# The first weight chunk in two halves, and a projection loop in which each tile's product stands ahead of a later tile's transposes

## The chip, the cores and the metric

The kernel runs on one core of a Trainium2 chip. The metric is the device time of one execution in microseconds, here of a single core. TensorE (PE in the rows) multiplies, VectorE (DVE) and ScalarE (ACT) work on the tiles elementwise, GpSimd (POOL) does small vectors and constants, and SyncE (SP) issues DMAs. Each engine runs its own instruction list in order and waits on semaphores.

## The reference, cut to what matters

The whole is one decoder layer with attention, an mLSTM and a mixture of experts. The change touches its first stage alone, the input projection:

```
def rmsnorm(x, w):
    y = xf * lax.rsqrt(jnp.mean(xf * xf, axis=-1, keepdims=True) + EPS)
    return y * w
xn = rmsnorm(x, p["attn_norm_w"])     # 1024 prompt tokens and 64 sample tokens, 1024 wide
proj = xn @ p["w_in"]                 # w_in: 1024 x 4872, float32; this stage makes 2824 columns of it
```

The product is made to float32 accuracy from operands split into a high part (rounded to the fp32r type) and a low part (the remainder): high by high, high by low, low by high are added up in one PSUM bank.

## The kernel before

`project` is the stage. The tokens are 9 tiles: tiles 0 to 7 of 128 prompt tokens, tile 8 of the 64 sample tokens. The weight comes in chunks of 352 columns (chunk 0 has 8 more, the gate columns, so 360) and 1024 rows, which are KD = 8 slices `k` of 128. Two sets of buffers (`w_ring`, `w_hi`, `w_lo`) alternate between chunks. Nothing plans the order: each engine's list is written out by hand in its block.

Per token tile t of chunk 0 these steps follow one another, each on its engine:

- ScalarE `square(t)` (L281), then GpSimd two short operations for the reciprocal root, then ScalarE `scale(t)` (L287) on the x tile.
- TensorE turns the tile: 8 transposes (L534), four into bank 6 and four into bank 7. I call this turn(t).
- VectorE `turned(t)` (L390, two instructions) multiplies both banks by the norm weight into `f_tile`.
- ScalarE `feat_hi(t)` (L291) casts to `f_hi`; VectorE `feat_lo(t)` (L402) subtracts for `f_lo`. Tile 8 has extra copies for `f_side` (L295, L401).
- TensorE product(t): 24 matmuls (L522 to L524, 8 slices by 3) of tile t with chunk 0 into PSUM bank t modulo 3. It first waits for `free` of that bank, which is only given back when the tile three before has been copied out by `evacuate` (L187 and L193, release at L198).

The copies out of chunk 0 are placed in the loops: ScalarE copies tile 0, 2, 4 in its passes t = 4, 6, 8 after `scale(t)`, VectorE tile 1 in its pass t = 5 and tile 3 in its pass t = 7, and both the rest after their loops. In a VectorE pass before: `turned(t)`, then `feat_lo(t - 1)`, then the copy, and in pass 7 then `split_lo(1)` (L408), the low part of chunk 1. ScalarE's pass is `square(t)`, `feat_hi(t - 1)`, `scale(t)`, the copy, and in pass 7 `split_hi(1)`.

TensorE's list before is turn(0), turn(1), turn(2), product(0), turn(3), product(1), and so on to turn(8), product(6), product(7), product(8). Seven more chunks of nine products follow, on two alternating sets of three banks. SyncE's list starts with x tiles 0 and 1, the norm weight, chunk 0 whole (L218), x tiles 2 to 8, chunk 1, and small loads.

Of the kernel before, what the change touches and what calls it, by code (L numbers as in the profile page):

```python
# [19 lines left out]
F32 = mybir.dt.float32  # L20
# [4 lines left out]
ALU = mybir.AluOpType  # L25
# [86 lines left out]
def project(nc, a, S):  # L112

    with ExitStack() as ctx:
# [62 lines left out]
        with nc.Block() as block:  # L177
# [37 lines left out]
            def _(sp):  # L215
                def load(n):
                    v = n % 2
                    sp.dma_start(w_ring[v][:, :, 0:width[n != 0]], w_view[:, :, columns(n, width[n != 0])]).then_inc(w_loaded[v], 16)  # L218
# [8 lines left out]
                for t in range(NT + 1):  # L227
                    src = xs if t == NT else a["x_prompt"][0, t * P:(t + 1) * P, :]
                    sp.dma_start(x_tile[t][:tile_rows(t)], src).then_inc(x_loaded[t], 16)
                    if t == 1:  # L230
                        sp.dma_start(S["attn_nw"][:], a["attn_norm_w"][0].rearrange("(k p) -> p k", p=P)).then_inc(norm_w_loaded, 16)
                        load(0)
                load(1)
                for dst, src in ((ib[:], a["mlstm_i_bias"].rearrange("o h -> h o")), (fb[:], a["mlstm_f_bias"].rearrange("o h -> h o")),
                                 (m0[:], a["state_m"][0].rearrange("b h -> h b")),
# [7 lines left out]
                spare = a["expert_rows"][(NE - 1) * SLOTS:MAXB * SLOTS, :].rearrange("(b s) d -> s b d", s=SLOTS)  # L243
                sp.wait_ge(zeros_ready, 1)
                for n in range(NCH - 2):
                    sp.wait_ge(w_lo_ready[n % 2], n // 2 + 1)
                    load(n + 2)
                    store(n)
                    if n in (1, 2):
                        half = slice((n - 1) * D // 2, n * D // 2)  # L250
                        sp.dma_start(spare[:, :, half], bc(zeros[:], 1, MAXB - NE + 1)).then_inc(spare_filled, 16)
# [1 line left out]
                sp.dma_start(a["row_c"], r_i[:]).then_inc(rows_stored, 16)  # L253
                sp.dma_start(a["m_prompt"][0, 0].rearrange("(h o) -> h o", o=1), r_m[:, TP - 1:TP]).then_inc(rows_stored, 16)
                sp.dma_start(a["m_sample"][0].rearrange("b h -> h b"), m_last[:, 8:16]).then_inc(rows_stored, 16)
                sp.wait_ge(w_lo_ready[0], NCH // 2)
                for j in range(2):
                    sp.dma_start(S["wg"][j][:], w_view[:, :, CG + j * P:CG + (j + 1) * P]).then_inc(wg_loaded[j], 16)
                store(NCH - 2)
# [17 lines left out]
            def _(act):  # L277
# [20 lines left out]
                def split_hi(n):  # L298
# [27 lines left out]
                square(1)  # L326
                scale(0)
                scale(1)
                feat_hi(0, P)
                split_hi(0)  # L330
                for t in range(2, NT + 1):
                    square(t)
                    feat_hi(t - 1, P)
# [43 lines left out]
            def _(dve):  # L377
# [26 lines left out]
                def split_lo(n):  # L404
                    cc, v = n // 2, n % 2
                    w = width[n != 0]
                    dve.wait_ge(w_hi_ready[v], cc + 1)
                    dve.tensor_tensor(w_lo[v][:, :, 0:w], w_ring[v][:, :, 0:w], w_hi[v][:, :, 0:w].bitcast(F32), ALU.subtract).then_inc(w_lo_ready[v], 1)  # L408

                rows = Own(dve, row_step)  # L410
                first = lambda ap: ap[:, TP:T:ST]
# [55 lines left out]
                            dve.tensor_copy(dst[:, :, q, :], src).then_inc(gcol_ready, 1)  # L467
                    dve.tensor_copy(S["wprev_all"][:], banks[7][:, 448:512]).then_inc(gcol_ready, 1)

                for t in range(NT + 1):  # L470
                    turned(t, tile_rows(t))
                    if t:
                        feat_lo(t - 1, P)
                    if t == 1:
                        split_lo(0)
                    if t in (5, 7):
                        evacuate(dve, 1, dve.tensor_copy, 0, only=t - 4)
                    if t == 7:
                        split_lo(1)
                feat_lo(NT, TS)  # L480
                for n in range(NCH):
                    if n == 3:
                        max_rows()
# [20 lines left out]
            def _(pe):  # L504
                pe.wait_ge(ms_ready, 6)

                def product(cc, v, t, w=CW):

                    b, r = 3 * v + t % 3, tile_rows(t)
                    pe.wait_ge(free[b], 3 * cc + t // 3 + 1)  # L510
                    if t == NT:
                        for k in range(KD):
                            if k:
                                pe.matmul(banks[b][:r, :w], f_hi[:, k, TP:T], w_lo[v][:, k, 0:w], start=False, stop=False)
                            ins = pe.matmul(banks[b][:, :w], f_side(slice(k, k + 1)).rearrange("p o t -> p (o t)"), w_hi[v][:, k, 0:w], start=(k == 0), stop=(k == KD - 1))
                            if k == 0:
                                pe.matmul(banks[b][:r, :w], f_hi[:, k, TP:T], w_lo[v][:, k, 0:w], start=False, stop=False)
                        ins.then_inc(full[b], 1)
                        return
                    for k in range(KD):  # L520
                        hi, lo = (f[:, k, t * P:t * P + r] for f in (f_hi, f_lo))
                        pe.matmul(banks[b][:r, :w], hi, w_hi[v][:, k, 0:w], start=(k == 0), stop=False)  # L522
                        pe.matmul(banks[b][:r, :w], hi, w_lo[v][:, k, 0:w], start=False, stop=False)  # L523
                        ins = pe.matmul(banks[b][:r, :w], lo, w_hi[v][:, k, 0:w], start=False, stop=(k == KD - 1))  # L524
                    ins.then_inc(full[b], 1)

                for t in range(NT + 1):
                    r = tile_rows(t)
                    pe.wait_ge(xn_ready, t + 1)
                    for h in range(2):  # L530
                        pe.wait_ge(xt_free[h], t + 1)
                        for k in range(4):
                            c = (4 * h + k) * P
                            ins = pe.transpose(banks[6 + h][:, k * P:k * P + r], x_tile[t][:r, c:c + P], S["ident"][:r, :r])  # L534
                        ins.then_inc(xt_full[h], 1)
                    if t >= 2:
                        if t == 2:
                            pe.wait_ge(w_lo_ready[0], 1)
                        pe.wait_ge(f_lo_ready, t - 1)
                        product(0, 0, t - 2, width[0])  # L540
                for t in range(NT - 1, NT + 1):
                    pe.wait_ge(f_lo_ready, t + 1)
                    product(0, 0, t, width[0])
# [2211 lines left out]
```

## Time and profile before

| | us |
|---|---|
| runs (3): median, lowest, highest | 1500.71, 1497.29, 1501.1 |
| the profiled execution: its own time | 1498.19 |
| its span, first to last instruction | 1496.4 |
| TensorE busy in it | 1415.3 (95%) |
| VectorE, ScalarE, GpSimd busy | 1003.0, 726.7, 210.4 |
| mean granted TensorE clock | 0.982 |

The span counts from the first to the last instruction, and the execution's own time has 1.8 us around it. The share of busy time is an average over stages; for a change in the first 60 us one reads the timeline of the engines there.

### The profile page before, as it was taken

How to read it: one execution, taken by the hardware profiler on the slowest of the kernel's cores; microseconds unless marked ns; L12 is line 12 of the kernel's file. 1: busy time of each engine (PE TensorE's matmuls, PEld its weight loads, DVE VectorE, ACT ScalarE, POOL GpSimd, SP SyncE). 2: the span in 40 equal slices, each digit the busy share in tenths (PEclk: the TensorE clock that was granted, in tenths of full speed). 3: DMA queues.
4: the chain of work that ended last, by engine and by line, in shares of the span. 5: the costliest groups of instructions: out<-in, count | busy, mean ns of one | idle time of the engine just before them, and what ended most of it. 6: DMA issues, size and time to landing. Idle time of an engine off the chain costs nothing.

```text
span 1496.4 us, 21540 instructions
## 1 busy us (share of the span) xinstructions
PE 1415.3 (95%) x8054; PEld 1198.2 (80%) x8054; DVE 1003.0 (67%) x1341; ACT 726.7 (49%) x861; POOL 210.4 (14%) x243
## 2 busy tenths in 40 slices
PE   5999999999999999999999889999999999999990
PEld 5999999998999998899788666777777777777760
DVE  4522321166666668776576688888888888888875
ACT  6421121144444444423212247777777777777760
POOL 2600000021111111000200040231111111111014
PEclk9999999999999999999999899999999999999995
DMA  6336423243333323658721289999999999999938
GB/s 200 120 123 212 147 79 70 76 136 109 119 124 114 115 73 108 190 179 252 282 92 42 97 332 392 365 380 399 394 390 391 390 390 393 396 393 399 379 126 319
DMA packets 135895, 347.40 MB, mean 232 GB/s; under 512 B 13768, under 2 KB 92044, under 8 KB 110160
## 3 DMA queue, kind: packets, MB, share of 16 engines
q1 hardware_dynamic: 125672, 312.32, 57.8%
q0 software_dynamic: 6048, 21.50, 4.7%
q10 hardware_dynamic: 4120, 12.85, 2.2%
q8 instruction: 34, 0.56, 0.2%
q14 instruction: 21, 0.17, 0.0%
HBM read 292.34 MB, written 55.28 MB: 232 GB/s over the span
## 4 chain that ended last, share of the span: by engine, by line
PE 45%; DVE 3%; DMA 1%; ACT 1%; issue 1%; POOL 0%; POOLq 0%; ACTq 0%; DVEq 0%
PE xt_ey L2560 4%; PE xt_ey L2561 4%; PE xt_ey L2562 4%; PE y_h_up L2539 4%; PE y_h_up L2538 4%; PE y_h_up L2540 4%; PE logits_gate L2538 2%; PE logits_gate L2540 2%; PE logits_gate L2539 2%; PE ranks_gate L2538 2%; PE ranks_gate L2540 2%; PE ranks_gate L2539 2%; PE y_x L2527 2%; DVE e_w_lo L2419 1%; PE y_x L2084 1%; PE y_h_up L2084 1%
## 5 line engine op out<-in xcount | busy, mean ns | idle before, releaser
L2419 DVE TENSOR_TENSOR e_w_lo<-mixed,e_w_hi 128x2048 fp32r<-128x2048 f32 x64 | 145.8, 2297 | 0.5 <-ACT e_w_hi L2352 0.5
L2419 DVE TENSOR_TENSOR e_w_lo<-w_out,e_w_hi 128x2048 fp32r<-128x2048 f32 x64 | 143.5, 2282 | 2.9 <-ACT e_w_hi L2352 2.9
L987 PE MATMUL gate_banks<-f_hi,wg_hi 128*128 128x364 f32 (+1 forms) x376 | 126.8, 337 | 0.9 <-DVE wg_lo L855 0.5
L2352 ACT CAST e_w_hi<-mixed 128x2048 fp32r<-128x2048 f32 x62 | 117.0, 1912 | 14.0 <-ACT e_y_rows L2373 8.9
L988 PE MATMUL gate_banks<-f_lo,wg_hi 128*128 128x364 f32 (+1 forms) x376 | 123.5, 328 | 0.0
L989 PE MATMUL gate_banks<-f_hi,wg_lo 128*128 128x364 f32 (+1 forms) x376 | 123.4, 328 | 0.0
L2352 ACT CAST e_w_hi<-w_out 128x2048 fp32r<-128x2048 f32 x64 | 121.8, 1904 | 0.6 <-ACT e_y_rows L2373 0.6
L2560 PE MATMUL xt_ey<-e_w_hi,e_hT_hi 128*96 128x512 f32 x256 | 103.5, 404 | 5.1 <-DVE e_w_lo L2419 3.9
L2279 POOL CAST idx<-token_of_slot 96x1 uint32 (+1 forms) x30 | 48.4, 1614 | 402.2 <-PE y_x L2527 368.9
L2561 PE MATMUL xt_ey<-e_w_lo,e_hT_hi 128*96 128x512 f32 x256 | 101.9, 398 | 0.0
L2538 PE MATMUL y_h_up<-e_w_hi,e_x_hi 128*96 128x512 f32 x256 | 100.8, 394 | 0.7 <-DVE e_w_lo L2419 0.7
L2562 PE MATMUL xt_ey<-e_w_hi,e_hT_lo 128*96 128x512 f32 x256 | 101.0, 395 | 0.0
L2539 PE MATMUL y_h_up<-e_w_lo,e_x_hi 128*96 128x512 f32 x256 | 100.8, 394 | 0.0
L2540 PE MATMUL y_h_up<-e_w_hi,e_x_lo 128*96 128x512 f32 x256 | 100.6, 393 | 0.0
L522 PE MATMUL gate_banks<-w_hi,f_hi 128*128 128x352 f32 (+1 forms) x256 | 84.1, 329 | 1.1 <-ACTq L198 1.1
L522 PE MATMUL pj<-w_hi,f_hi 128*128 128x352 f32 x256 | 82.7, 323 | 1.8 <-ACTq L198 1.8
L524 PE MATMUL gate_banks<-w_hi,f_lo 128*128 128x352 f32 (+1 forms) x256 | 83.4, 326 | 0.0
L523 PE MATMUL gate_banks<-w_lo,f_hi 128*128 128x352 f32 (+1 forms) x256 | 83.3, 326 | 0.0
L523 PE MATMUL pj<-w_lo,f_hi 128*128 128x352 f32 x256 | 82.9, 324 | 0.0
L524 PE MATMUL pj<-w_hi,f_lo 128*128 128x352 f32 x256 | 82.7, 323 | 0.0
L2419 DVE TENSOR_TENSOR e_w_lo<-w_gate,e_w_hi 128x2048 fp32r<-128x2048 f32 x32 | 72.9, 2280 | 1.2 <-ACT e_w_hi L2352 1.2
L2419 DVE TENSOR_TENSOR e_w_lo<-w_up,e_w_hi 128x2048 fp32r<-128x2048 f32 x32 | 71.9, 2287 | 0.1
(626 smaller groups left out, 3604.6 us busy)
## 6 DMA issues: line engine op xcount, KB each, us to landing
w_out<-in_w_down_e SPq DMA_DIRECT2D x64, 1024.0 KB, 8.0
mixed<-in_w_gate_e SPq DMA_DIRECT2D x32, 1024.0 KB
mixed<-in_w_up_e SPq DMA_DIRECT2D x32, 1024.0 KB, 8.4
w_gate<-in_w_gate_e SPq DMA_DIRECT2D x32, 1024.0 KB, 7.2
w_up<-in_w_up_e SPq DMA_DIRECT2D x32, 1024.0 KB
expert_rows<-e_y_rows ACTq DMA_DIRECT2D x32, 384.0 KB, 7.3
proj<-mixed SPq DMA_DIRECT2D x8, 1408.0 KB, 5.6
w_ring<-in_w_in SPq DMA_DIRECT2D x7, 1408.0 KB, 10.7
```

The lines of the kernel that those rows point to most:

```text
L522: pe.matmul(banks[b][:r, :w], hi, w_hi[v][:, k, 0:w], start=(k == 0), stop=False)
L523: pe.matmul(banks[b][:r, :w], hi, w_lo[v][:, k, 0:w], start=False, stop=False)
L524: ins = pe.matmul(banks[b][:r, :w], lo, w_hi[v][:, k, 0:w], start=False, stop=(k == KD - 1))
L987: pe.matmul(bank, wg_hi[j][:, k, :], hi, start=(k == 0), stop=False)
L2352: act.copy(hi(i, step, j), raw(i, u, j)).then_inc(hi_ready[i], 1)
L2419: dve.tensor_tensor(lo(i, u, j), raw(i, u, j), hi(i, step, j).bitcast(F32), ALU.subtract).then_inc(lo_ready[i], 1)
L2538: pe.matmul(bank[:SLOTS, :], x_hi[u][:, k, :], w_hi[:, n, :], start=(k == 0), stop=False)
L2539: pe.matmul(bank[:SLOTS, :], x_hi[u][:, k, :], w_lo[:, n, :], start=False, stop=False)
L2540: ins = pe.matmul(bank[:SLOTS, :], x_lo[u][:, k, :], w_hi[:, n, :], start=False, stop=(k == KD - 1))
L2560: pe.matmul(Y[:SLOTS, cols], h_hi[:, f, :], w_hi[:, n, cols], start=(f == 0), stop=False)
L2561: pe.matmul(Y[:SLOTS, cols], h_hi[:, f, :], w_lo[:, n, cols], start=False, stop=False)
L2562: ins = pe.matmul(Y[:SLOTS, cols], h_lo[:, f, :], w_hi[:, n, cols], start=False, stop=(f == KF - 1))
```

## The change

Four edits, all in chunk 0 of the projection.

1. SyncE loads chunk 0 as two DMAs, k slices 0 to 3 and 4 to 7, the first with a semaphore of its own. ScalarE and VectorE split it by the same halves. The counts of the semaphores for buffer set 0 go up by one, because chunk 0 now signals twice.
2. ScalarE's list starts scale(1), first half of `w_hi`, `feat_hi(0)`, second half. Its loop is unchanged.
3. VectorE: tile t's `feat_lo` now follows its own `turned(t)` in the same pass. The copies of tile 1 and tile 3 stay in passes 5 and 7, behind it.
4. TensorE: product(t) now stands ahead of turn(t + 2), and product(0) waits for the halves of `w_lo` at k = 0 and k = 4.

```diff
+        FIRST_HALVES = (slice(0, KD // 2), slice(KD // 2, KD))
...
                     if t == 1:
                         sp.dma_start(S["attn_nw"][:], a["attn_norm_w"][0].rearrange("(k p) -> p k", p=P)).then_inc(norm_w_loaded, 16)
-                        load(0)
+                        for i, ks in enumerate(FIRST_HALVES):
+                            sp.dma_start(w_ring[0][:, ks, 0:width[0]], w_view[:, ks, columns(0, width[0])]).then_inc(w_loaded[0] if i else first_half_loaded, 16)
...
+                def first_split_hi(i):
+                    ks = FIRST_HALVES[i]
+                    act.wait_ge(w_loaded[0] if i else first_half_loaded, 16)
+                    act.copy(w_hi[0][:, ks, 0:width[0]], w_ring[0][:, ks, 0:width[0]]).then_inc(w_hi_ready[0], 1)
...
                 scale(1)
+                first_split_hi(0)
                 feat_hi(0, P)
-                split_hi(0)
+                first_split_hi(1)
                 for t in range(2, NT + 1):
...
+                def first_split_lo(i):
+                    ks = FIRST_HALVES[i]
+                    dve.wait_ge(w_hi_ready[0], i + 1)
+                    dve.tensor_tensor(w_lo[0][:, ks, 0:width[0]], w_ring[0][:, ks, 0:width[0]], w_hi[0][:, ks, 0:width[0]].bitcast(F32), ALU.subtract).then_inc(w_lo_ready[0], 1)
...
-                for t in range(NT + 1):
+                turned(0, P)
+                first_split_lo(0)
+                feat_lo(0, P)
+                first_split_lo(1)
+                turned(1, P)
+                feat_lo(1, P)
+                for t in range(2, NT + 1):
                     turned(t, tile_rows(t))
-                    if t:
-                        feat_lo(t - 1, P)
-                    if t == 1:
-                        split_lo(0)
+                    feat_lo(t, tile_rows(t))
                     if t in (5, 7):
                         evacuate(dve, 1, dve.tensor_copy, 0, only=t - 4)
                     if t == 7:
                         split_lo(1)
-                feat_lo(NT, TS)
...
                     for k in range(KD):
+                        if first and k % (KD // 2) == 0:
+                            pe.wait_ge(w_lo_ready[0], k // (KD // 2) + 1)
...
-                    if t >= 2:
-                        if t == 2:
-                            pe.wait_ge(w_lo_ready[0], 1)
-                        pe.wait_ge(f_lo_ready, t - 1)
-                        product(0, 0, t - 2, width[0])
+                turn_x(0)
+                turn_x(1)
+                for t in range(NT - 1):
+                    pe.wait_ge(f_lo_ready, t + 1)
+                    product(0, 0, t, width[0], t == 0)
+                    turn_x(t + 2)
                 for t in range(NT - 1, NT + 1):
                     pe.wait_ge(f_lo_ready, t + 1)
                     product(0, 0, t, width[0])
```

TensorE at the start, from turn(1) on (banks pj6 and pj7 take the transposes, the gate banks the products). Before:

```order
L534 MATMUL pj6<-ident,mixed 128x128 [waits xt_free0,xn_ready]
L534 MATMUL pj6<-ident,mixed 128x128 x3
L534 MATMUL pj7<-ident,mixed 128x128 [waits xt_free1]
L534 MATMUL pj7<-ident,mixed 128x128 x3
L534 MATMUL pj6<-ident,mixed 128x128 [waits xt_free0,xn_ready]
L534 MATMUL pj6<-ident,mixed 128x128 x3
L534 MATMUL pj7<-ident,mixed 128x128 [waits xt_free1]
L534 MATMUL pj7<-ident,mixed 128x128 x3
L522 MATMUL gate_banks<-w_hi0,f_hi_49 128x360 [waits pj_free0,f_lo_ready,w_lo_ready0]
```

The same place in the changed kernel:

```order
L553 MATMUL pj6<-ident,mixed 128x128 [waits xt_free0,xn_ready]
L553 MATMUL pj6<-ident,mixed 128x128 x3
L553 MATMUL pj7<-ident,mixed 128x128 [waits xt_free1]
L553 MATMUL pj7<-ident,mixed 128x128 x3
L541 MATMUL gate_banks<-w_hi0,f_hi_49 128x360 [waits w_lo_ready0,pj_free0,f_lo_ready]
```

Turn(2) has moved from ahead of product(0) to behind it.

VectorE's first instructions (early holds `f_tile`). Before:

```order
L390 TENSOR_TENSOR early<-pj6,attn_nw 128x512 [waits xt_full0,norm_w_loaded]
L390 TENSOR_TENSOR early<-pj7,attn_nw 128x512 [waits xt_full1]
L390 TENSOR_TENSOR early<-pj6,attn_nw 128x512 [waits xt_free1,xt_full0]
L390 TENSOR_TENSOR early<-pj7,attn_nw 128x512 [waits xt_full1]
L402 TENSOR_TENSOR f_lo_50<-early,f_hi_49 128x8x128 [waits xt_free1,f_hi_ready]
L408 TENSOR_TENSOR w_lo0<-w_ring0,w_hi0 128x2880 [waits w_hi_ready0]
```

Changed:

```order
L400 TENSOR_TENSOR early<-pj6,attn_nw 128x512 [waits xt_full0,norm_w_loaded]
L400 TENSOR_TENSOR early<-pj7,attn_nw 128x512 [waits xt_full1]
L423 TENSOR_TENSOR w_lo0<-w_ring0,w_hi0 128x1440 [waits xt_free1,w_hi_ready0]
L412 TENSOR_TENSOR f_lo_50<-early,f_hi_49 128x8x128 [waits f_hi_ready]
L423 TENSOR_TENSOR w_lo0<-w_ring0,w_hi0 128x1440 [waits w_hi_ready0]
L400 TENSOR_TENSOR early<-pj6,attn_nw 128x512 [waits xt_full0]
L400 TENSOR_TENSOR early<-pj7,attn_nw 128x512 [waits xt_full1]
```

Tile 0 is finished, and both halves of the weight's low part made, before tile 1's banks are read.

TensorE around product(4), which needs bank 1 back from tile 1 (`pj_free1`). Before, what stands ahead of it is turn(6):

```order
L524 MATMUL gate_banks<-w_hi0,f_lo_50 128x360
L534 MATMUL pj6<-ident,mixed 128x128 [waits xt_free0,xn_ready]
L534 MATMUL pj6<-ident,mixed 128x128 x3
L534 MATMUL pj7<-ident,mixed 128x128 [waits xt_free1]
L534 MATMUL pj7<-ident,mixed 128x128 x3
L522 MATMUL gate_banks<-w_hi0,f_hi_49 128x360 [waits pj_free1,f_lo_ready]
```

Changed, it is turn(5):

```order
L543 MATMUL gate_banks<-w_hi0,f_lo_50 128x360
L553 MATMUL pj6<-ident,mixed 128x128 [waits xt_free0,xn_ready]
L553 MATMUL pj6<-ident,mixed 128x128 x3
L553 MATMUL pj7<-ident,mixed 128x128 [waits xt_free1]
L553 MATMUL pj7<-ident,mixed 128x128 x3
L541 MATMUL gate_banks<-w_hi0,f_hi_49 128x360 [waits pj_free1,f_lo_ready]
```

Every product stands one turn earlier in TensorE's list than before. VectorE's pass 5, which reads turn(5) and then copies out tile 1, is in the changed kernel:

```order
L400 TENSOR_TENSOR early<-pj6,attn_nw 128x512 [waits xt_full0,f_lo_ready]
L400 TENSOR_TENSOR early<-pj7,attn_nw 128x512 [waits xt_full1]
L412 TENSOR_TENSOR f_lo_50<-early,f_hi_49 128x8x128 [waits xt_free1,f_hi_ready]
L190 COPY mixed<-gate_banks 128x352 [waits pj_full1]
L196 COPY if_tok_73<-gate_banks 128x2x4
```

Before it has the same five forms in this pass, but its f_lo is that of tile 4; now it is that of tile 5, whose banks the two instructions ahead of it have just read.

## Rows read from the trace of the kernel before

**Rows 1.** The page: busy time, share and instructions of each engine.

```profile
PE 1415.3 (95%) x8054; PEld 1198.2 (80%) x8054; DVE 1003.0 (67%) x1341; ACT 726.7 (49%) x861; POOL 210.4 (14%) x243
```

**Rows 2.** Timeline, TensorE: start us, length us, instruction [idle before <-releaser].

```profile
8.57 3.98 PE L534 MATMUL pj<-ident,mixed 128*128 128x128 f32 x16 [8.57 <-ACT mixed L287]
19.97 1.97 PE L534 MATMUL pj<-ident,mixed 128*128 128x128 f32 x8 [7.42 <-ACT mixed L287]
21.59 0.65 PE L522 MATMUL gate_banks<-w_hi,f_hi 128*128 128x360 f32 x1
...
23.49 0.33 PE L522 MATMUL gate_banks<-w_hi,f_hi 128*128 128x360 f32 x1
```

**Rows 3.** Timeline, TensorE: turn(3), product(1), turn(4).

```profile
26.47 1.04 PE L534 MATMUL pj<-ident,mixed 128*128 128x128 f32 x8
27.26 0.41 PE L522 MATMUL gate_banks<-w_hi,f_hi 128*128 128x360 f32 x1
...
31.29 1.04 PE L534 MATMUL pj<-ident,mixed 128*128 128x128 f32 x8
```

**Rows 4.** Timeline, TensorE: turn(7), turn(8), product(6).

```profile
45.77 1.03 PE L534 MATMUL pj<-ident,mixed 128*128 128x128 f32 x8
...
51.06 0.71 PE L534 MATMUL pj<-ident,gate_rows 64*128 64x64 f32 x8 [0.30 <-ACT gate_rows L287]
51.70 0.43 PE L522 MATMUL gate_banks<-w_hi,f_hi 128*128 128x360 f32 x1
```

**Rows 5.** DMA issues of the first 25 us: KB, median us from issue to landing.

```profile
w_ring<-in_w_in SPq DMA_DIRECT2D x1, 1440.0 KB, 8.5
```

**Rows 6.** Timeline, ScalarE, 0 to 75 us.

```profile
11.33 1.04 ACT L291 CAST f_hi<-early 128x1024 fp32r<-128x1024 f32 x1 [1.82 <-DVEq L395]
12.28 2.59 ACT L304 CAST w_hi<-w_ring 128x2880 fp32r<-128x2880 f32 x1
...
28.62 1.05 ACT L291 CAST f_hi<-early 128x1024 fp32r<-128x1024 f32 x1 [2.67 <-DVEq L395]
29.57 1.15 ACT L287 ACTIVATE mixed<-mixed,x_rstd 128x1024 f32<-128x1024 f32 x1
...
48.72 1.05 ACT L291 CAST f_hi<-early 128x1024 fp32r<-128x1024 f32 x1
...
55.01 0.71 ACT L295 CAST f_side<-early 128x448 fp32r<-128x448 f32 x2 [0.70 <-DVE f_lo L402]
```

**Rows 7.** Timeline, VectorE, 0 to 75 us.

```profile
9.77 1.47 DVE L390 TENSOR_TENSOR early<-pj,attn_nw 128x512 f32<-128x512 f32 x2 [9.77 <-PE pj L534]
...
13.43 1.23 DVE L402 TENSOR_TENSOR f_lo<-early,f_hi 128x1024 fp32r<-128x1024 f32 x1 [0.15 <-DVE early L390]
14.90 3.16 DVE L408 TENSOR_TENSOR w_lo<-w_ring,w_hi 128x2880 fp32r<-128x2880 f32 x1 [0.24 <-ACT w_hi L304]
...
27.18 1.29 DVE L390 TENSOR_TENSOR early<-pj,attn_nw 128x512 f32<-128x512 f32 x2 [3.14 <-PE pj L534]
...
39.42 0.52 DVE L187 COPY mixed<-gate_banks 128x352 f32<-128x352 f32 x1
...
47.93 1.23 DVE L402 TENSOR_TENSOR f_lo<-early,f_hi 128x1024 fp32r<-128x1024 f32 x1 [0.15 <-DVE early L390]
...
49.84 3.09 DVE L408 TENSOR_TENSOR w_lo<-w_ring,w_hi 128x2816 fp32r<-128x2816 f32 x1 [0.18 <-DVE if_tok L193]
52.85 0.75 DVE L390 TENSOR_TENSOR early<-pj,attn_nw 128x256 f32<-128x256 f32 x2
...
56.64 0.68 DVE L402 TENSOR_TENSOR f_lo<-early,f_hi 128x512 fp32r<-128x512 f32 x1
```

**Rows 8.** Timeline, TensorE: the first matmul after a wait.

```profile
721.85 0.47 PE L2073 MATMUL y_x<-w_out_hi,first_merged_hi 128*128 128x512 f32 x1 [2.49 <-PEq L103]
```

**Rows 9.** Windows: length, PE, PEld, DVE, ACT, POOL busy, clock, DMA.

```profile
720.00:724.00 4.00, 2.15 (x8) 1.77 (x9) 1.75 (x3) 2.17 (x3) 1.98 (x10) 0.90 0.15 7
724.00:728.00 4.00, 4.00 (x14) 3.18 (x13) 4.00 (x5) 3.61 (x4) 3.46 (x9) 0.68 0.78 165
```

More of the change, by code:

```diff
@@ L156, in project @@
         w_loaded = [sem(f"w_loaded{v}") for v in range(2)]
+        first_half_loaded = sem("first_half_loaded")
         full = [sem(f"pj_full{b}") for b in range(6)]
@@ L245, in _ @@
                 for n in range(NCH - 2):
-                    sp.wait_ge(w_lo_ready[n % 2], n // 2 + 1)
+                    sp.wait_ge(w_lo_ready[n % 2], n // 2 + 2 - n % 2)
                     load(n + 2)
@@ L255, in _ @@
                 sp.dma_start(a["m_sample"][0].rearrange("b h -> h b"), m_last[:, 8:16]).then_inc(rows_stored, 16)
-                sp.wait_ge(w_lo_ready[0], NCH // 2)
+                sp.wait_ge(w_lo_ready[0], NCH // 2 + 1)
                 for j in range(2):
@@ L406, in split_lo @@
                     w = width[n != 0]
-                    dve.wait_ge(w_hi_ready[v], cc + 1)
+                    dve.wait_ge(w_hi_ready[v], cc + 2 - v)
                     dve.tensor_tensor(w_lo[v][:, :, 0:w], w_ring[v][:, :, 0:w], w_hi[v][:, :, 0:w].bitcast(F32), ALU.subtract).then_inc(w_lo_ready[v], 1)
+                def first_split_lo(i):
+                    ks = FIRST_HALVES[i]
+                    dve.wait_ge(w_hi_ready[0], i + 1)
+                    dve.tensor_tensor(w_lo[0][:, ks, 0:width[0]], w_ring[0][:, ks, 0:width[0]], w_hi[0][:, ks, 0:width[0]].bitcast(F32), ALU.subtract).then_inc(w_lo_ready[0], 1)
                 rows = Own(dve, row_step)
@@ L505, in _, with product @@
                 pe.wait_ge(ms_ready, 6)
-                def product(cc, v, t, w=CW):
+                def product(cc, v, t, w=CW, first=False):
                     b, r = 3 * v + t % 3, tile_rows(t)
@@ L525, in product, with turn_x @@
                     ins.then_inc(full[b], 1)
-                for t in range(NT + 1):
+                def turn_x(t):
                     r = tile_rows(t)
@@ L553, in _ @@
                     for v in range(2):
-                        pe.wait_ge(w_lo_ready[v], cc + 1)
+                        pe.wait_ge(w_lo_ready[v], cc + 2 - v)
                         for t in range(NT + 1):
@@ L557, in _ @@
                 for v in range(2):
-                    pe.wait_ge(w_lo_ready[v], NCH // 2)
+                    pe.wait_ge(w_lo_ready[v], NCH // 2 + 1 - v)
                     for t in range(NT + 1):
```

## The prediction

> **What bounds the kernel now.** I read the page first: TensorE is busy for 95% of the span [rows 1]. What the change can give or take is therefore time in which TensorE stands still in the first 64 us, since every later stage is fed by buffers that TensorE's own progress sets free; a shift of its list there should arrive at the end at full size. Next the timeline of TensorE. Turn(0) and turn(1) run from 8.57 to 12.55, then it idles 7.42 us until scale(2) on ScalarE lets turn(2) start at 19.97; product(0) starts at 21.59 [rows 2]. From then on it is nearly full: turn(3) starts at 26.47, product(1) at 27.26, turn(4) at 31.29, so in steady state a turn takes 0.79, a product 4.03 and a step of both 4.82 us [rows 3]. Turn(8) waits 0.30 us and takes 0.64 [rows 4].
>
> **The gain at the start.** ScalarE ends scale(1) at 9.5, the end of the piece ahead of the row at 11.33. The whole chunk lands about 8.5 us after its issue at 2.2, so at 10.7 [rows 5]; the landing of its first half no row shows. It is at the latest 10.7; at an even rate over the 2.5 MB of x tiles 0 and 1 and the chunk, its 1.8 MB would be there near 8. I take anything before 9.5, when ScalarE comes free. Half of `w_hi` costs 1.39 us, by the line through 1.04 us for 1024 elements and 2.59 for 2880 [rows 6], half of `w_lo` 1.66 by 1.23 and 3.16 [rows 7]. Walk: first `w_hi` half 9.5 to 10.9; `turned(0)` 9.77 to 11.24 [rows 7]; `feat_hi(0)` 11.33 to 12.4, second `w_hi` half to 13.7; on VectorE first `w_lo` half 11.3 to 13.0, `feat_lo(0)` 12.9 to 14.15, second half 14.1 to 15.7, `turned(1)` 15.7 to 17.1. So product(0) starts at 14.2, not 21.59, and its k = 4 wait, 3.6 us in, finds the half of 15.7 done. If the first half landed only at 10.7, product(0) would start at 15.0: 0.8 us less gain.
>
> Its length: before, 6 of its first pitches fill 21.59 to 23.49 at about 0.30 us, and after 23.49 they are 0.165 (18 to 26.47) [rows 2, 3]; that is 1.2 against 2.4 GHz, and the faster level came 3.5 us after turn(2) began. The same 3.5 us from 14.2 on gives 11 slow matmuls, and 13 fast ones end at 19.9. At the slow level throughout it would end at 21.6, so 0 to 1.7 us are open; I take 19.9, as the row is the only ramp there is here. Scale(2) stands behind `feat_hi(1)` (17.1 to 18.15) and ends at 19.2, so turn(2) does not wait. Turn(3) then starts at 19.9 + 0.79 + 4.03 = 24.7. Before, at 26.47, TensorE had product(1) still to do; so it is 1.8 + 4.0 = 5.8 us ahead.
>
> **The steady step.** `turned(t)` starts 0.71 after turn(t) (27.18 against 26.47), `feat_hi(t)` 2.15 after it (28.62), scale(t + 1) ends 4.25 after it (29.57 + 1.15) [rows 3, 6, 7]. Now `feat_lo(t)` follows `feat_hi(t)`: start at 3.23, end at 4.46, and product(t), which needs it, is due at 4.82 + 0.79 = 5.61. Both fit. The extra DMA issue (about 0.5 us of SyncE) delays x tiles 2 to 8 and the small loads behind it; what covers it is that scale(2) has over 2 us of slack behind `feat_hi(1)`. Uncovered it would cost 0.5. The two more instructions on ScalarE and VectorE are in the walk.
>
> **Where the lead is lost: the bank handed back late.** Product(4) needs bank 1, which VectorE releases in pass 5 after copying out tile 1. Before, product(4) stands behind turn(6), and the copy ran at 39.42, behind `feat_lo(4)` [rows 7], while turn(6) began only at 31.29 + 2 x 4.82 = 40.9. Changed, product(4) stands behind turn(5), and the copy behind `feat_lo(5)`, which cannot start before turn(5) + 3.23. From the start of a `feat_lo` to the release is 1.91 us (47.93 to 49.84, with the same copies in pass 7) [rows 7]. So bank 1 is free at turn(5) + 5.15, product(4) starts at 5.2 and was due at 0.79: **4.4 us of standing still**. The queue behind it on TensorE is all the rest, and VectorE and ScalarE can't shorten it, since what they wait for is turn(5) itself.
>
> Product(6) needs bank 0 from tile 3, copied in pass 7 behind `feat_lo(7)`. Here ScalarE does chunk 1's `w_hi` and square(8) ahead of `feat_hi(7)`, which starts 2.95 after turn(7) (48.72 against 45.77) [rows 4, 6]. `Feat_lo(7)` starts at 4.03, the release is at 5.94, product(6) starts at 6.0 and was due at 0.79: **5.2 us**. Turn(8) waits no more: 0.3 us back.
>
> Product(8) needs bank 2 from tile 5, which VectorE copies after `feat_lo(8)`. `Split_lo(1)` (3.1 us) ends at turn(7) + 9.0, before turn(8) is through, so `turned(8)` starts at turn(8) + 0.4. From there to the start of `feat_lo(8)` were 3.79 us (52.85 to 56.64), of which 0.70 was a wait that has gone [rows 6, 7]; `feat_lo(8)` is 0.55 shorter, so the release comes 3.09 + 1.36 later, at turn(8) + 4.85 and 0.1 to act. Product(8) was due at 0.64 + 4.03 = 4.67: **0.3 us**, with bounds 0 and 1.
>
> **The sum at full clock.** Turn(5) at 24.7 + 2 x 4.82 = 34.4; product(4) 39.6; turn(7) 39.6 + 4.03 + 4.82 = 48.4; product(6) 54.4; turn(8) 58.4; product(7) 59.1; product(8) 63.4. Before, product(8) began at 51.70 + 2 x 4.03 = 59.8 [rows 4]. So +3.6 us (-5.8 + 4.4 + 5.2 + 0.3 - 0.3 and rounding).
>
> **The clock after a standstill.** At 721.85 TensorE resumes after a wait of 2.49 us, and the granted clock of the two 4 us windows there is 0.90 and 0.68 [rows 8, 9]. Between levels 1 and 0.5 that is 0.8 + 2.6 = 3.4 us at 1.2 GHz, almost all while it worked, half of it lost: 1.6 us. The standstills of 4.4 and 5.2 us are longer, so I charge 1.6 for each, +3.2; bounds 0 and 3.2. The second is not hidden by the first: each slow stretch lies inside the product that follows its wait, and the next wait is counted from a turn behind it. The sum is +3.6 + 3.2 = +6.8 us.
>
> The Trainium skill, "TensorE: Matmul & The Clock Gate", "What's actually happening", says that "the default state is throttled, and activity releases the throttle". By that rule a bubble costs more than its length, which speaks against this change; without it the sum would be +3.6, with it +6.8. The trace agrees at its wait of 2.49 us, with a clock of 0.68 behind it.
>
> **Against the runs.** The profiled execution took 1498.19 us, its span 1496.4; the median is 1500.71, 2.5 above the former. The difference carries over: 1498.2 + 6.8 = 1505.0 for such an execution, 1507.5 for the median. About 0.3%, 4.5 us, is what a measurement of this kernel can tell from no change.
>
> **Cases.**
> - A, forecast, 0.62: both waits with their slow stretches, +6.8: 1507.5.
> - B, 0.17: the waits are as worked out, but the clock stays at 2.4 GHz after one or both, or the falls are short: +3.6 to +5.2, near 1505. For it: TensorE has been working densely up to each wait. Against it: the fall behind 2.49 us.
> - C, 0.10: the start gains less, because the first half lands late (0.8) or product(0) runs at 1.2 GHz throughout (1.7), or a slow stretch is longer: +8 to +10, near 1509.5.
> - D, the other side, 0.08: the bank handover does not decide, because the releases come within 0.8 us of turn(5) and turn(7). That needs the copy of tile 1 to run ahead of `feat_lo(5)`, and it decides at a release before turn + 0.8. Then product(6) is due at 24.7 + 4 x 4.82 + 0.79 = 44.8, product(7) at about 49.9, and product(8) still waits for `feat_lo(8)`, which `split_lo(1)` holds back to some 13.3 after turn(7) (9.0 + 4.3), so to 57.3 against 59.8: -2.5, 1498.2. Even then most of the 5.8 us is given back. The order of VectorE's list speaks against it.
> - E, 0.03: the whole lead reaches the end, -5.8: 1494.9. It needs D and no wait at product(8).
>
> Faster by over 0.3% is E: 0.03. Within 0.3% are D and half and more of B with a little of A: 0.23. Slower by over 0.3%: 0.74. The range takes in B and C: from +2 to +11 us with the scatter of the medians, 1502.5 to 1511.5.
>
> **What would show it.** In the changed profile: product(0) near 14.2 and turn(3) near 24.7; TensorE idle about 4.4 us behind turn(5), released by VectorE's release behind the copy of tile 1, and about 5.2 us behind turn(7); matmul pitches of 0.30 us behind both and a granted clock under 1 there; the first matmul of product(8) near 66.6. A TensorE timeline without idle between 20 and 60 us would make it wrong, as would a later stage in which the delay shrinks.

## The result

The changed kernel took 1508.32 us (median of 5 runs, 1506.24 to 1511.57), the kernel before 1499.02 (5 runs, 1497.29 to 1501.1). The ratio is 1.0057, with a 95% interval of 1.0046 to 1.0068: slower by 8.5 us (6.9 to 10.2). The two medians lie 9.3 us apart; the differences below go by the ratio. The profiled execution took 1508.32 us, its span 1506.6, which is 10.2 above the span before.

The page of the changed kernel, to be held against [rows 1]:

```profile
PE 1423.9 (95%) x8054; PEld 1205.8 (80%) x8054; DVE 1001.5 (66%) x1342; ACT 726.3 (48%) x862; POOL 220.8 (15%) x243
```

TensorE is busy for as large a share as before, with the same 8054 matmuls, and 8.6 us longer. That is the first sign that it not only stood still but ran slower. The timeline of TensorE (start us, length us, instruction, idle before it and who ended it), against [rows 2 to 4], first the start:

```profile
14.21 0.67 PE L541 MATMUL gate_banks<-w_hi,f_hi 128*128 128x360 f32 x1 [1.69 <-DVE f_lo L412]
14.68 0.50 PE L542 MATMUL gate_banks<-w_lo,f_hi 128*128 128x360 f32 x1
...
18.22 0.33 PE L542 MATMUL gate_banks<-w_lo,f_hi 128*128 128x360 f32 x1
...
20.04 1.04 PE L553 MATMUL pj<-ident,mixed 128*128 128x128 f32 x8
```

Product(0) begins at 14.21 in place of 21.59. Its matmuls are 0.30 us apart up to 17.98 and 0.165 from 18.22 on. Turn(2) follows at once at 20.04. Then turn(3), turn(5) and product(4):

```profile
24.88 1.04 PE L553 MATMUL pj<-ident,mixed 128*128 128x128 f32 x8
...
34.53 1.03 PE L553 MATMUL pj<-ident,mixed 128*128 128x128 f32 x8
39.72 0.64 PE L541 MATMUL gate_banks<-w_hi,f_hi 128*128 128x360 f32 x1 [4.16 <-DVEq L201]
```

Turn(6), turn(7) and product(6), whose releaser is the same:

```profile
46.34 1.03 PE L553 MATMUL pj<-ident,mixed 128*128 128x128 f32 x8
...
51.16 1.04 PE L553 MATMUL pj<-ident,mixed 128*128 128x128 f32 x8
57.14 0.64 PE L541 MATMUL gate_banks<-w_hi,f_hi 128*128 128x360 f32 x1 [4.95 <-DVEq L201]
```

Turn(8), product(7), product(8), and the first matmul of chunk 1:

```profile
63.69 0.71 PE L553 MATMUL pj<-ident,gate_rows 64*128 64x64 f32 x8
...
68.70 0.40 PE L532 MATMUL gate_banks<-w_hi,f_side 128*128 128x360 f32 x1 [0.17 <-DVEq L201]
...
71.40 0.32 PE L541 MATMUL pj<-w_hi,f_hi 128*128 128x352 f32 x1
```

In the kernel before, that last row was:

```profile
62.32 0.32 PE L522 MATMUL pj<-w_hi,f_hi 128*128 128x352 f32 x1
```

So chunk 1 begins 9.1 us later. Who was waited for, by TensorE in the first 85 us (total us, times, longest us):

```profile
PE gate_banks L541 <- DVEq L201: 9.1, 2, 4.9
...
PE gate_banks L532 <- DVEq L201: 0.2, 1, 0.2
```

L201 is the release of a bank on VectorE. The two waits of 4.2 and 4.9 us stand ahead of product(4) and product(6), the one of 0.2 us ahead of product(8).

The windows of the changed kernel (stretch, length, busy time of PE, PEld, DVE, ACT and POOL, granted clock, DMA share, GB/s), against [rows 9]:

```profile
12.00:16.00 4.00, 2.31 (x9) 1.91 (x8) 4.00 (x4) 2.70 (x4) 1.15 (x2) 1.00 1.03 412
36.00:40.00 4.00, 0.28 (x1) 0.31 (x2) 2.27 (x4) 3.19 (x5) 0.00 (x0) 0.83 0.00 0
40.00:44.00 4.00, 4.00 (x14) 4.00 (x14) 0.00 (x0) 0.46 (x2) 0.74 (x2) 0.50 0.00 0
44.00:48.00 4.00, 4.00 (x24) 3.97 (x24) 0.95 (x2) 0.00 (x0) 0.00 (x0) 0.82 0.00 0
52.00:56.00 4.00, 0.19 (x2) 0.00 (x0) 1.98 (x3) 3.97 (x5) 1.71 (x5) 0.96 0.00 0
56.00:60.00 4.00, 2.86 (x10) 2.89 (x11) 3.82 (x4) 0.59 (x3) 3.84 (x3) 0.50 0.87 273
60.00:64.00 4.00, 4.00 (x21) 3.77 (x21) 0.19 (x1) 0.00 (x0) 3.62 (x6) 0.69 0.27 94
```

With each wait the granted clock is at its lower level for 6.8 us: 0.17 of 4 us twice over, then a whole 4 us, then 0.18 twice over make 1.4 + 4.0 + 1.4, and the second fall likewise 0.3 + 4.0 + 2.5. Counted back from the whole windows, the clock fell at about 38.6 and 55.7, so that some 1.1 and 1.5 us of the low stretches lay still inside the waits, which ended at 39.72 and 57.14. Product(4) takes 6.62 us up to turn(6), product(6) 6.55 up to turn(8); the steady product took 4.03 [rows 3].

VectorE (against [rows 7]), then ScalarE (against [rows 6]), at the places of the sum:

```profile
11.36 1.66 DVE L423 TENSOR_TENSOR w_lo<-w_ring,w_hi 128x1440 fp32r<-128x1440 f32 x1
12.94 1.22 DVE L412 TENSOR_TENSOR f_lo<-early,f_hi 128x1024 fp32r<-128x1024 f32 x1
...
37.76 1.23 DVE L412 TENSOR_TENSOR f_lo<-early,f_hi 128x1024 fp32r<-128x1024 f32 x1 [1.22 <-ACT f_hi L295]
38.90 0.52 DVE L190 COPY mixed<-gate_banks 128x352 f32<-128x352 f32 x1
39.33 0.16 DVE L196 COPY if_tok<-gate_banks 128x8 f32<-128x8 f32 x1
...
55.18 1.22 DVE L412 TENSOR_TENSOR f_lo<-early,f_hi 128x1024 fp32r<-128x1024 f32 x1 [2.02 <-ACT f_hi L295]
```

```profile
9.39 1.38 ACT L313 CAST w_hi<-w_ring 128x1440 fp32r<-128x1440 f32 x1
```

The first half of `w_hi` starts at 9.39, with no idle time ahead, so the half had landed; the first half of `w_lo` runs 11.36 to 13.0 and `feat_lo(0)` at 12.94. The release of bank 1 comes after `feat_lo(5)` at 37.76 and the copies at 38.90 and 39.33, and TensorE starts at 39.72, within 0.3 us. `Feat_lo(7)` starts at 55.18, 4.02 us after turn(7) as forecast.

### The profile page after: what moved, and what is told of

Its sections match the earlier page's. It is cut to its first block, busy times and chain, and to the rows that moved or that the text cites. A ratio compares the mean times of both kernels' runs of the same rounds, so it can differ in the third digit from the quotient of the medians.

```text
span 1506.6 us, 21545 instructions
## 1 busy us (share of the span) xinstructions
PE 1423.9 (95%) x8054; PEld 1205.8 (80%) x8054; DVE 1001.5 (66%) x1342; ACT 726.3 (48%) x862; POOL 220.8 (15%) x243
## 4 chain that ended last, share of the span: by engine, by line
PE 45%; DVE 3%; DMA 1%; ACT 1%; issue 1%; POOL 0%; POOLq 0%; ACTq 0%; DVEq 0%
PE xt_ey L2581 4%; PE xt_ey L2582 4%; PE xt_ey L2583 4%; PE y_h_up L2560 4%; PE y_h_up L2559 4%; PE y_h_up L2561 4%; PE logits_gate L2559 2%; PE logits_gate L2561 2%; PE logits_gate L2560 2%; PE ranks_gate L2559 2%; PE ranks_gate L2561 2%; PE ranks_gate L2560 2%; PE y_x L2548 2%; DVE e_w_lo L2440 1%; PE y_x L2105 1%; PE y_h_up L2105 1%
## 5 line engine op out<-in xcount | busy, mean ns | idle before, releaser
L541 PE MATMUL gate_banks<-w_hi,f_hi 128*128 128x352 f32 (+1 forms) x256 | 87.0, 340 | 11.9 <-DVEq L201 9.1
L1008 PEld LDWEIGHTS gate_banks<-f_hi,wg_hi 128*128 128x128 f32 x376 | 70.7, 188 | 1.6 <-issue 1.4
```

The lines of the kernel that those rows point to most:

```text
L1008: pe.matmul(bank, wg_hi[j][:, k, :], hi, start=(k == 0), stop=False)
```

## Experiments

All are timed against the kernel before in alternating rounds. The last column is the ratio less 1, times 1499 us. The column ahead of it compares the first recorded matmul of chunk 1 with that of before (62.32) in one profiled execution each. (A matmul record can be missing from a trace, so these starts may be a pitch or two of 0.16 us late.)

| kernel | chunk 1 starts | against before | ratio (95%) | us by the runs |
|---|---|---|---|---|
| changed | 71.40 | +9.1 | 1.0057 (1.0046 to 1.0068) | +8.5 |
| e1 | 60.48 | -1.8 | 0.9983 (0.9970 to 0.9996) | -2.5 |
| e2 | 61.86 | -0.5 | 0.9991 (0.9980 to 1.0002) | -1.3 |
| e3 | 65.83 | +3.5 | 1.0019 (1.0009 to 1.0029) | +2.8 |
| e4 | 74.22 | +11.9 | 1.0084 (1.0065 to 1.0102) | +12.6 |
| e5 | 56.01 | -6.3 | 0.9964 (0.9951 to 0.9978) | -5.4 |
| e6 | 68.86 | +6.5 | 1.0045 (1.0031 to 1.0059) | +6.7 |
| e7 | 56.21 | -6.1 | 0.9952 (0.9938 to 0.9966) | -7.2 |

The two columns agree within 1.1 us for all eight: what TensorE gains or loses before chunk 1 arrives at the end at full size.

**e1: the copies one pass earlier.**

```diff
-                    if t in (5, 7):
-                        evacuate(dve, 1, dve.tensor_copy, 0, only=t - 4)
+                    if t in (4, 6):
+                        evacuate(dve, 1, dve.tensor_copy, 0, only=t - 3)
```

> The changed kernel with VectorE's copies of tile 1 and tile 3 in passes 4 and 6 in place of 5 and 7. Theory (the bank is handed back too late): both TensorE waits of 4.2 and 5.0 us ahead of product(4) and product(6) go, and the slow matmuls behind them with them. A smaller one opens ahead of product(8), since feat_lo(8) and the copy of tile 5 still stand behind split_lo(1): product(8) starts near 56.9 in place of 59.8 before and 68.7 in the changed kernel. Time against before: -2.9 us, up to -0.3 if the clock falls at that wait. Rival (the waits come from something else than the copy's place, such as feat_lo itself): they stay, and the time is +8 us or so against before.

Both waits and the slow products behind them are gone; product(4) and product(6) follow their turns at once, and one wait is left:

```profile
56.34 0.64 PE L532 MATMUL gate_banks<-w_hi,f_side 128*128 128x360 f32 x1 [2.83 <-DVEq L201]
```

It stands ahead of product(8). VectorE shows why:

```profile
48.73 3.29 DVE L418 TENSOR_TENSOR w_lo<-w_ring,w_hi 128x2816 fp32r<-128x2816 f32 x1
51.94 0.74 DVE L400 TENSOR_TENSOR early<-pj,attn_nw 128x256 f32<-128x256 f32 x2
...
55.52 0.51 DVE L190 COPY mixed<-gate_banks 128x352 f32<-128x352 f32 x1
```

`Split_lo(1)` at 48.73 holds `turned(8)` back to 51.94, and the copy of tile 5 comes last, at 55.52. Two lines on VectorE are worth 11 us by the runs. The rival, that the waits come from elsewhere, is out. The number lies inside the forecast span of -2.9 to -0.3. The clock did fall at the wait that is left (granted clock 0.57 from 56 to 60 us): product(8) starts 3.5 us earlier than before, chunk 1 only 1.8.

**e2: TensorE's old order, the rest as changed.**

```diff
                 for t in range(NT - 1):
+                    turn_x(t + 2)
                     pe.wait_ge(f_lo_ready, t + 1)
                     product(0, 0, t, width[0], t == 0)
-                    turn_x(t + 2)
```

> The changed kernel with TensorE's old order alone: turn(t + 2) ahead of product(t). Halves and VectorE's tile by tile order stay. Theory (TensorE's order takes the slack away, VectorE's order alone costs nothing): no wait above 0.5 us after 25 us; turn(2) starts near 19.2 in place of 19.97, since scale(2) comes earlier; -0.7 us against before. Rival (VectorE's new order, with feat_lo behind its own turned, is itself a cost): waits remain ahead of some product and the time is 1 us or more above before.

```profile
19.30 1.97 PE L553 MATMUL pj<-ident,mixed 128*128 128x128 f32 x8 [6.70 <-ACT mixed L291]
...
51.26 0.40 PE L541 MATMUL gate_banks<-w_hi,f_hi 128*128 128x360 f32 x1 [0.18 <-DVEq L201]
```

Turn(2) starts at 19.30, and behind it the only wait before chunk 1 that the profile lists is 0.18 us ahead of product(6); turn(8) comes some 0.3 us late besides (0.5 us in the kernel before). VectorE's tile by tile order costs nothing while every product stands behind a second turn. The gain of 1.3 us (interval from 3.0 faster to 0.3 slower) can't be told from the 0.7 forecast, nor from none.

**e3: work put into the two waits.** 24 and 28 matmuls are added, into a bank that chunk 1 overwrites.

```diff
                     pe.wait_ge(f_lo_ready, t + 1)
+                    if t in (4, 6):
+                        for k in range(24 if t == 4 else 28):
+                            pe.matmul(banks[3][:, :CW], f_hi[:, k % KD, 0:P], w_hi[0][:, k % KD, 0:CW], start=True, stop=True)
                     product(0, 0, t, width[0], t == 0)
```

> The changed kernel with 24 matmuls of 352 columns added ahead of product(4) and 28 ahead of product(6), into a bank that is unused until chunk 1 overwrites it: 4.0 and 4.6 us of extra work inside the waits of 4.2 and 5.0 us. Theory (the products behind the waits are slow because the clock falls while TensorE stands still): product(4) and product(6) take 4.0 us and not 6.6, granted clock 1 there, product(8) starts near 63.6 in place of 68.7; 5 us less than the changed kernel, +3.5 us against before. Rival (something else slows those products, or the price of the fall was 1.6 each as forecast): no gain, or 3.2 us.

Product(4) with the turn behind it, and product(6) with its own:

```profile
39.23 0.43 PE L541 MATMUL gate_banks<-w_hi,f_hi 128*128 128x360 f32 x1 [0.22 <-DVEq L201]
...
43.28 1.04 PE L553 MATMUL pj<-ident,mixed 128*128 128x128 f32 x8
```

```profile
54.01 0.43 PE L541 MATMUL gate_banks<-w_hi,f_hi 128*128 128x360 f32 x1 [0.37 <-DVEq L201]
...
58.16 0.71 PE L553 MATMUL pj<-ident,gate_rows 64*128 64x64 f32 x8
```

Both start as late as in the changed kernel, counted from turn(5) and turn(7) (5.1 and 5.9 us), and take 4.05 and 4.15 us, in place of 6.62 and 6.55; the granted clock of every 4 us window from 36 to 60 us that holds them is 1.00. So the two falls of the clock cost 2.6 and 2.4 us, which is 5.0 of the 5.6 us by which chunk 1 begins earlier than in the changed kernel; the rest is the start (0.4) and releases that come 0.2 us sooner. The runs give 5.7 us less than the changed kernel (2.8 against 8.5, with about 2 us either way by the two intervals), for 52 matmuls more. The forecast of 1.6 is out as a price for these waits.

**e4: the first chunk whole.**

```diff
-                        for i, ks in enumerate(FIRST_HALVES):
-                            sp.dma_start(w_ring[0][:, ks, 0:width[0]], w_view[:, ks, columns(0, width[0])]).then_inc(w_loaded[0] if i else first_half_loaded, 16)
+                        load(0)
...
-                first_split_hi(0)
                 feat_hi(0, P)
-                first_split_hi(1)
+                act.wait_ge(w_loaded[0], 16)
+                act.copy(w_hi[0][:, :, 0:width[0]], w_ring[0][:, :, 0:width[0]]).then_inc(w_hi_ready[0], 2)
...
-                first_split_lo(0)
                 feat_lo(0, P)
-                first_split_lo(1)
+                dve.wait_ge(w_hi_ready[0], 2)
+                dve.tensor_tensor(w_lo[0][:, :, 0:width[0]], w_ring[0][:, :, 0:width[0]], w_hi[0][:, :, 0:width[0]].bitcast(F32), ALU.subtract).then_inc(w_lo_ready[0], 2)
```

> The changed kernel with the first weight chunk loaded and split whole: one DMA, one w_hi cast behind feat_hi(0), one w_lo subtraction behind feat_lo(0). Orders otherwise as changed. Theory (the halves bring the first product forward): product(0) starts near 18.1 in place of 14.2, everything after it 3.9 us later, +12.4 us against before. Rival (scale(2) or the clock's ramp sets the pace of the start anyway): less than 1.5 us above the changed kernel, +8.5 to +10 against before.

```profile
17.95 0.64 PE L540 MATMUL gate_banks<-w_hi,f_hi 128*128 128x360 f32 x1 [5.73 <-DVE w_lo L487]
...
23.33 1.03 PE L552 MATMUL pj<-ident,mixed 128*128 128x128 f32 x8
```

Product(0) at 17.95 is 3.7 us later than in the changed kernel, turn(2) at 23.33 3.3 us, and chunk 1 at 74.22 2.8 us. By the runs e4 is 4.1 us slower than the changed kernel, with about 3 us either way, so the +12.6 against before agrees with the 12.4 forecast. Loading by halves is worth about what product(0) comes earlier. The rival of under 1.5 us is out by the traces; the runs alone would not quite exclude it.

**e5: the third release too.** On top of e1, tile 5 is copied in pass 7, and chunk 1's low part comes behind tile 8.

```diff
-                    if t in (4, 6):
-                        evacuate(dve, 1, dve.tensor_copy, 0, only=t - 3)
-                    if t == 7:
+                    if t in (4, 6, 7):
+                        evacuate(dve, 1, dve.tensor_copy, 0, only={4: 1, 6: 3, 7: 5}[t])
+                    if t == NT:
                         split_lo(1)
...
-                    evacuate(dve, 1, dve.tensor_copy, n, 0 if n else 4)
+                    evacuate(dve, 1, dve.tensor_copy, n, 0 if n else 6)
```

> As e1 (copies of tile 1 and 3 one pass earlier), and VectorE copies tile 5 in pass 7 and makes chunk 1's low part (split_lo(1)) behind feat_lo(8) in place of ahead of turned(8). Theory (the third hand-back, ahead of product(8), is late because split_lo(1) and tile 8 stand ahead of tile 5's copy): the wait of 2.8 us that e1 showed there goes; chunk 1's first matmul at about 56.5 in place of 62.3 before, 71.4 changed, 60.3 in e1; -5.8 us against before. Rival (the wait only moves to chunk 1, whose low part now comes later): chunk 1 starts above 58.5, and the time is within 1.5 us of e1.

Turn(2), and the first matmul of chunk 1:

```profile
18.80 1.10 PE L553 MATMUL pj<-ident,mixed 128*128 128x128 f32 x8 [0.77 <-ACT mixed L291]
```

```profile
56.01 0.43 PE L541 MATMUL pj<-w_hi,f_hi 128*128 128x352 f32 x1 [0.32 <-DVE w_lo L418]
```

Turn(2) has to wait 0.77 us for scale(2) here, because product(0) ran faster in this execution (see the last section). The wait ahead of product(8) is gone, and chunk 1 waits 0.32 us for its low part.

It is 5.4 us faster than before by the runs (3.3 to 7.3), against 5.8 forecast: within that interval the lead of 5.8 us arrives once no release is late. The earlier copy of tile 5 and the later low part were moved together, so what each is worth by itself is not shown. The rival, a wait that only moves to chunk 1, is out.

**e6: the waits filled by half.**

```diff
+                    if t in (4, 6):
+                        for k in range(12):
+                            pe.matmul(banks[3][:, :CW], f_hi[:, k % KD, 0:P], w_hi[0][:, k % KD, 0:CW], start=True, stop=True)
```

> The changed kernel with 12 extra matmuls ahead of product(4) and 12 ahead of product(6), half of what filled the waits in e3, so that waits of about 2.2 and 3.0 us are left. Question: why each fall cost 2.6 us in the changed kernel and not the 1.6 forecast from the wait of 2.49 us. Theory (the length of the low stretch follows from how long TensorE stood still, 6.8 us behind 4.2 and 5.0 us of it): the waits left here bring low stretches of at most 3.4 us each, products of at most 5.7 us, and the time lies 2 us or more under the changed kernel, +4 to +6 against before. Rival (a fall here costs 2.6 us whatever the length of the wait): products of 6.6 us again, +8.5 against before.

Product(4) and turn(6), then the windows:

```profile
39.17 0.50 PE L541 MATMUL gate_banks<-w_hi,f_hi 128*128 128x360 f32 x1 [2.14 <-DVEq L201]
...
44.80 1.03 PE L553 MATMUL pj<-ident,mixed 128*128 128x128 f32 x8
```

```profile
36.00:40.00 4.00, 1.86 (x10) 1.57 (x9) 1.81 (x4) 3.64 (x6) 0.00 (x0) 0.92 0.00 0
40.00:44.00 4.00, 4.00 (x18) 4.00 (x18) 0.00 (x0) 0.01 (x1) 0.74 (x2) 0.65 0.00 0
...
56.00:60.00 4.00, 4.00 (x17) 4.00 (x16) 2.65 (x1) 0.00 (x0) 3.78 (x4) 0.57 0.87 324
```

Waits of 2.14 and 2.94 us are left, and both still bring the clock down, but the low stretches are 3.4 us each (0.6 + 2.8 and 3.4) and the products take 5.63 and 5.68 us. That is 1.6 us above 4.03, the forecast's price. So the longer low stretch came with the longer wait, as the theory has it, and the rival of 2.6 whatever the wait is out. In time the kernel lies 1.8 us under the changed one and 6.7 above before (4.6 to 8.8), where at least 2 and at most 6 had been expected; the intervals can't tell these apart.

**e7: chunk 1 in quarters.** On top of e5; the semaphore counts for buffer set 1 go up by three.

```diff
-                    if t == 7:
-                        split_hi(1)
+                    if 3 <= t <= 6:
+                        ks = slice(2 * (t - 3), 2 * (t - 2))
+                        act.wait_ge(w_loaded[1], 16)
+                        act.copy(w_hi[1][:, ks, 0:CW], w_ring[1][:, ks, 0:CW]).then_inc(w_hi_ready[1], 1)
...
                     turned(t, tile_rows(t))
+                    if 4 <= t <= 7:
+                        ks = slice(2 * (t - 4), 2 * (t - 3))
+                        dve.wait_ge(w_hi_ready[1], t - 3)
+                        dve.tensor_tensor(w_lo[1][:, ks, 0:CW], w_ring[1][:, ks, 0:CW], w_hi[1][:, ks, 0:CW].bitcast(F32), ALU.subtract).then_inc(w_lo_ready[1], 1)
                     feat_lo(t, tile_rows(t))
-                    if t == NT:
-                        split_lo(1)
```

> As e5, but chunk 1 is split in quarters of two k slices: ScalarE casts one in each of passes 3 to 6, VectorE subtracts one in each of passes 4 to 7 between turned(t) and feat_lo(t), where it idles 1.2 us. Theory: square(8) and scale(8) come earlier, turn(8) no longer waits 0.3 us, nothing waits at chunk 1: chunk 1's first matmul 0.3 to 0.6 us earlier than in e5, about -6.3 us against before. Rival (a quarter of 0.85 us on VectorE and 0.8 on ScalarE does not fit the idle time of a pass, and feat_lo(t) or scale(t + 1) comes too late for TensorE): waits of up to 1 us in several passes and a slower kernel than e5.

VectorE in pass 5: a quarter and `feat_lo(5)`. Then TensorE's turn(8) and chunk 1:

```profile
36.47 0.89 DVE L499 TENSOR_TENSOR w_lo<-w_ring,w_hi 128x704 fp32r<-128x704 f32 x1
37.55 1.23 DVE L415 TENSOR_TENSOR f_lo<-early,f_hi 128x1024 fp32r<-128x1024 f32 x1 [0.19 <-ACT f_hi L296]
```

```profile
48.89 0.71 PE L558 MATMUL pj<-ident,gate_rows 64*128 64x64 f32 x8
...
56.21 0.32 PE L546 MATMUL pj<-w_hi,f_hi 128*128 128x352 f32 x1
```

The quarter of 0.89 us fits, `feat_lo(5)` starts 0.19 us after it, and TensorE has no wait between product(0) and chunk 1. From turn(2) to chunk 1 it takes 36.4 us (19.83 to 56.21), in e5 37.2 (18.80 to 56.01). Chunk 1 itself did not begin 0.3 to 0.6 us earlier than in e5, as expected, but 0.2 later, because turn(2) came 1.0 us later in this execution. This is the fastest kernel of the study, 0.9952 of before (0.9938 to 0.9966), against 1.0057 for the changed one. That it beats e5 (0.9964) the intervals don't show.

## Why the prediction was right, and where it was off

- **The number.** Forecast +6.8 us, measured +8.5. In absolute terms 1507.5 and 1508.32 lie closer, 0.8 us apart, but that is partly luck: the forecast stood on a median before of 1500.71, and the five runs gave 1499.02.
- **The case.** The two late releases and a slow stretch behind each are case A. That the slow stretches were longer than charged stood only in case C, held at 0.10 ("or a slow stretch is longer: +8 to +10"), and the +8.5 falls there.
- **The start.** Product(0) 14.2 forecast, 14.21 found; turn(2) 19.9 and 20.04; turn(3) 24.7 and 24.88. The half landed before 9.4. The extra DMA issue put the issue of x tile 2 from 2.79 to 3.65, more than the 0.5 us taken, and it stayed hidden. That product(0) ended so near the forecast is partly chance: in other executions of the same orders the clock rose and fell at other moments, and product(0) took 4.2 (e5) or 5.6 us (e1, e6, e7) in place of 5.8. The 3.7 us by which e4 delays product(0) reach chunk 1 for the most part (2.8).
- **The steady step.** Held: no wait ahead of product(1) to product(3), and `feat_lo(5)` starts 3.23 us after turn(5) (37.76 against 34.53).
- **The bank handed back late.** Product(4) forecast at 39.6, found at 39.72; product(6) at turn(7) + 6.0, found at + 5.98 (57.14 against 51.16); product(8) 0.3 us late, found 0.17. Product(8) itself starts at 68.70 and not at 66.6, almost wholly because of the two longer slow stretches (1.0 us each). e1 takes the cause away and both waits go; this is shown.
- **The product(8) limit.** Case D said that even with both releases in time product(8) would start near 57.3 and give -2.5 us. e1 is that case: product(8) starts at 56.34, 1.0 us earlier than worked out there, and a slow stretch behind its wait of 2.83 us, which case D did not charge, takes 1.6 us back. That the runs too say -2.5 us is therefore luck in part; the trace of e1 says -1.8 at chunk 1.
- **The clock.** This is the term that was mis-sized, and its bounds were wrong as well. The sum charged 1.6 us for each fall, "bounds 0 and 3.2", from one wait of 2.49 us. Found: 2.6 and 2.5 us against the steady product, 5.0 for both against e3. So the 5 us for both fell outside the bounds of 0 to 3.2. The weak step is that a price read at a wait of 2.49 us was carried over to waits of 4.2 and 5.0 us as if it did not grow: the low stretch was 6.8 us and not 3.4, with 1.1 to 1.5 us of it inside the wait, where it costs nothing. e6 shows the price of 1.6 where the waits are 2.1 and 2.9 us. With 2.6 in its place the sum is +8.8 us, and the runs gave +8.5. The row itself was one of two outcomes: the same wait of 2.49 us brought no fall in e3 and e5 to e7 (see the last section).
- **One more fall.** In the profile of the changed kernel the clock also falls near 601.8 us for 3.4 us (0.73 and 0.85 in the windows 600 to 604 and 604 to 608), behind a wait of 2.22 us that was 2.03 us long in the kernel before and brought no fall. It costs nothing in the end: the delay against before grows from 9.2 to 10.7 us within it and is back at 9.2 us behind it, because there the kernel before waits 1.34 us and the changed one does not. The last 1.0 us of the 10.2 in the span comes later, half of it near 864 us of the kernel before, where the clock is low for 13.7 us in that kernel and for 17.0 in the changed one; no single cause for it is shown.

The Trainium skill says in "TensorE: Matmul & The Clock Gate", "What's actually happening", that the default is the throttled state, and the prediction read from it that a bubble (TensorE standing still) costs more than its length. The runs agree in direction: e3, which fills the bubbles with useless work, is 5.7 us faster than the kernel without it.

## What to carry to other kernels

When a consumer is moved one step earlier in an in-order list, every buffer it waits for must be handed back one step earlier too: list each `free` it needs and the pass of the other engine in which that release stands. Cost a bubble on TensorE at its length plus the slow stretch behind it, and don't take the latter from a shorter bubble. Here the reorder, with the first chunk in halves, was sound and worth 5 to 7 us (e5, e7); three copies that had stayed in their old places, and one long subtraction ahead of the last of them, turned it into a loss of 8.5.

## What the runs showed of the hardware that was not expected

- In the projection (the first 75 us) the low stretch behind a wait for a bank came in two lengths: 3.4 us behind waits of 2.14, 2.83 and 2.94 us (e6, e1), 6.8 us behind waits of 4.15 to 4.95 us, in the four falls of the changed kernel and e4. For a wait of 3 to 4 us the traces give no clean answer. The only one, of 3.03 us near 850 us in all nine traces, has the clock low for 13.7 to 17.0 us, but TensorE works there only part of the time (2.06 of 4 us in the window 848 to 852 of the kernel before).
- A short wait does not always bring a fall. The wait of 2.49 us of [rows 8] stands in all nine traces. In five (before, changed, e1, e2, e4) the clock was low for 3.4 us there, in four (e3, e5, e6, e7) it stayed up. A wait of 1.78 us near 206 us brought 3.4 us in e5, and the same wait (1.79 us, near 212) brought none in the kernel before; one of 2.06 us brought a fall in e4, and one of 2.21 us none in e5. So at these lengths a fall is a cost that some executions have and others don't; what decides it no run here shows. In e5, the windows at the wait of 1.78 us, which ended at 206.21, and at that of 2.49 us, which ended at 717.35:

```profile
204.00:208.00 4.00, 2.22 (x11) 1.93 (x10) 0.00 (x0) 2.52 (x5) 0.00 (x0) 0.88 0.00 0
208.00:212.00 4.00, 4.00 (x19) 4.00 (x19) 0.08 (x1) 0.00 (x0) 0.00 (x0) 0.69 0.00 0
...
716.00:720.00 4.00, 2.65 (x12) 2.20 (x13) 1.77 (x3) 2.68 (x3) 2.41 (x11) 1.00 0.27 27
720.00:724.00 4.00, 4.00 (x19) 3.27 (x18) 4.00 (x4) 3.12 (x4) 3.53 (x8) 1.00 0.68 198
```

- The granted clock in the window 12 to 16 us of the changed kernel reads 1.00, while the matmuls there are 0.30 us apart, the pitch of the lower level. At this program's start the column can't be relied on; the pitch can.
- In e1 and e5 to e7 the first matmuls of product(0) are 0.16 us apart, so the clock had risen before 14 us. In e1, e6 and e7 the pitch goes to 0.30 us again from about 15 us on, for 3.4 us, and product(0) took 5.6 us there against 5.8 in the changed kernel. In e2 the clock fell during the wait ahead of turn(2) (0.54 from 16 to 20 us). In e5 it did not fall, product(0) was through by 18.0 and turn(2) waited 0.77 us for `scale(2)`. The orders up to that point are the same in the changed kernel, e1 and e5, so it varies from one execution to the next; why stays open.
